# The entry into the decode loop and the order of its chunks, in a one-core layer of prompt and decode

## The chip, the cores and the metric

The kernel runs on one core of one Trainium2 chip. The time is the device time of a run in microseconds, as the median of several runs. Everything is float32.

## The reference, cut to what matters

One transformer layer is run for a prompt of 1024 tokens and for 8 decode sequences of 4 new tokens each with 2048 cached tokens. The heads are of two kinds: heads with a compressed, a selected and a window branch (NSA), and heads with a latent cache (MLA). The part that the change touches is the decode attention; the rest (projection, prompt attention, output projection) is around it.

```
full = concat([cache_nsa[page_table], kv_new])        # per sequence, 2048 + 4 rows of 4 x 2 x 64
kc, vc = compress(full[0], w_ck), compress(full[1], w_cv)    # 32 rows -> 1, every 16 rows
s   = q . kc * scale + bias;  p_c = softmax(s);  o_cmp = p_c . vc
imp = p_c . overlap;  idx = top_k(imp with forced blocks, 16)       # blocks of 64 rows
o_sel = softmax(q . k_selected + bias) . v_selected
o_win = softmax(q . [state_win, k_new] + bias) . [state_win_v, v_new]
o_lat = softmax(q_lat . ckv + q_rope . k_rope) . ckv   # latent cache, 2048 + 4 rows of 192
out = x + gate * (concat([(g0 o_cmp + g1 o_sel + g2 o_win) silu(z_a), (o_lat w_uv) silu(z_b)]) @ w_out)
y = rmsnorm(out) * g_final
```

## The kernel before, in words

The kernel is one program for five engines, each with its own instruction stream: TensorE (PE), VectorE (DVE), ScalarE (ACT), GpSimd (POOL) and SyncE (SP, which issues nearly all DMAs). The order on each engine is written out by hand, and engines wait for each other on semaphores only. An engine that waits holds up everything behind the wait in its own stream.

**The stages.** Projection of all tokens, preparation, prompt attention, the output projection of the eight prompt tiles (`pe_out`, `act_out`, `dve_out`, `pool_out`, `sp_out`, tiles m = 0 to 7), the decode loop over the sequences b = 0 to 7 (`pe_decode_loop` with its helpers, `act_decode`, `dve_decode`, `pool_decode`, `sp_decode`), and the output projection of the decode rows (`..._out_sample`).

**Output projection of a tile.** PE multiplies 32 blocks (L1609, two halves c of 512 columns, banks 2 to 5), DVE multiplies by the gate (L1692) and adds x (L1695), ACT squares and sums the row (L1672), POOL takes the inverse root (L1707, L1710), DVE scales (L1698), and SP stores the tile (L1577, the last tile L1581). In tiles 5, 6 and 7 PE also turns the first six of eight chunks of the first decode sequence (L1613). In this stage SP issues the loads that decode needs (L1559 to L1574).

**Chunks.** The keys and values to be compressed of one sequence are 16 pages of 128 rows. PE transposes four pages at a time into a PSUM bank (`chunk`, L1820: K0 to K3 for keys, V0 to V3 for values), and ACT or DVE copies the bank into `XT` (`read_chunk`, L2126; for ACT L2131 is the copy lambda, in the output stage L1662). The chunks K0, K2, V0, V2 are read by ACT, the others by DVE. In the loop, chunks of sequence b+1 and seven small results of sequence b (`cmp`, `pts`, `fmw`, `imp`, `smw`, `fs`, `ss`) go round three PSUM banks 0 to 2 in the order of `RING`; `next_bank` makes PE wait until the item three places back has been read. The first eight chunks use banks 6 and 7 in turn, with the wait two places back.

**One round of PE** (sequence b): `compress` of the keys (64 matmuls, L1965, banks 3 and 4), `window_scores` (L1978), `compressed_scores` (L1988), `latent_scores` 0 to 4 (L2000), `probabilities` (L2020 to L2022), `latent_scores` 4 to 6 (L2000, then L2004 to L2006), `compress` of the values 0 to 5, the sum over partitions `fmw` (L2031), `importance` (L2027), `compress` 5 to 16, `smw` (L2031), `selected_scores` (L2013), `latent_values` (L2037, L2041), `window_values` (L2048, L2049), `compressed_values` (L2054), K0 of b+1, `fs` (L2031), K1, K2, `ss` (L2031), K3, V0, V1, `selected_values` (L2059, L2061), V2, V3.

**One round of DVE.** It copies the output of the round before (L2204), turns the window keys into `KWT` (L2210) and the selected keys into `KT4` (L2215), subtracts masks from the window scores (L2222 to L2224), takes minima and spreads them (L2227, L2178; semaphore `s_nm` releases the sums `fmw` and `fs`), normalises the compressed probabilities (L2234 to L2236), copies `pts` (L2242), ranks blocks (L2252 to L2264), scales and turns probabilities (L2181, L2270, L2272), reads the compressed values (L2275), masks and reduces the selected scores (L2281 to L2287), reads `fs` (L2290), K1 (L2126), the latent result (L2294) and `ss` (L2297), scales and turns the selected probabilities into `PTS` (L2300), reads K3 and V1, turns the latent cache in three parts (`latent_turns`, L2173: `MLT0` to `MLT2`), and reads V3.

**The entry into decode.** Behind the output projection PE waits for both gated halves of the last tile (L1947), then turns V2 and V3 and compresses. `window_scores` of b = 0 waits for `KWT` turned, the query copies built by POOL (`QB`, L2364) and all late loads:

```
                if b == 0:
                    pe.wait_ge(s_late, LATE)
```

These late loads (`load_late`, L1872 to L1890) are 17 DMAs behind the last store: new keys into `KWT` (L1875), a mask (`NCBF`, L1879), `NEWM` (L1881), and the new values `VN` (L1886 to L1890). They wait for memsets that POOL does after the last tile (L2344 to L2346). DVE clears small tiles and adds two masks (L2183 to L2198), turns the latent cache, reads V3, and only then turns the window keys. SP reads the page numbers of b = 1 (`page_numbers`, a load of 16 registers, L1897) and issues its 16 pages (L1905) after the late loads.

## Time and profile before

| | us |
|---|---|
| median of three runs | 1207.02 (1205.22 to 1209.93) |
| the profiled execution, own time | 1206.63 |
| its span | 1204.9 |
| PE busy in the span | 1145.6 (95%) |
| DVE busy | 547.0 (45%) |
| ACT busy | 314.3 (26%) |
| GpSimd busy | 86.6 (7%) |

PE is the engine that is nearly always busy; the ends of its matmuls are modelled, so the start times of successive instructions are the surer reading. The output projection ends at 931 us on the clock of the span, the decode rounds run from 938 to 1190 us, about 30.6 us each.

### The profile page before, as it was taken

Reading aid. Unit: us, or ns where it says so; the run is one execution under the profiler, and the core shown is the slowest. Engines: PE = TensorE matmul, PEld = TensorE weight load, DVE = VectorE, ACT = ScalarE, POOL = GpSimd, SP = SyncE. Lnnn points to the kernel's source line nnn. Section 1 sums busy time; section 2 is a strip of 40 time slices with the busy share of each in tenths; the row PEclk is TensorE's granted clock in tenths of the full one; section 3 lists DMA queues with packets and bytes.
Section 4 is the critical chain, followed back from the end, with each engine's and each line's share of the span. In section 5 each row is a group of like instructions: output and inputs, shape, how many; then the busy total and the mean of one; then the engine's idle time right before and its main releaser. Section 6 shows DMA issues by size and latency. Waiting matters only on the chain.

```text
span 1204.9 us, 20843 instructions
## 1 busy us (share of the span) xinstructions
PE 1145.6 (95%) x7894; PEld 773.4 (64%) x7894; DVE 547.0 (45%) x1421; ACT 314.3 (26%) x636; POOL 86.6 (7%) x209
## 2 busy tenths in 40 slices
PE   5899999999999999998999999989999799999997
PEld 2576767444444667776888787864444576666665
DVE  0211110111111467767665655632333577777774
ACT  0212110101111356545443344420111122222220
POOL 0000000000000011101000000010000200000000
PEclk9799999999999989999999999999999899999998
DMA  9665212000003160000000000003961487666660
GB/s 346 258 204 145 106 35 85 10 7 4 3 7 42 32 164 2 2 1 2 1 1 1 1 1 1 2 12 110 211 222 52 159 266 260 225 221 226 222 180 19
DMA packets 83306, 115.94 MB, mean 96 GB/s; under 512 B 30113, under 2 KB 52052, under 8 KB 82184
## 3 DMA queue, kind: packets, MB, share of 16 engines
q1 hardware_dynamic: 83208, 114.61, 30.0%
q8 instruction: 64, 1.05, 0.4%
q14 instruction: 34, 0.28, 0.1%
HBM read 102.31 MB, written 12.27 MB: 95 GB/s over the span
## 4 chain that ended last, share of the span: by engine, by line
PE 81%; issue 8%; DVE 5%; DMA 3%; ACT 1%; SPq 1%; POOL 1%; POOLq 0%; DVEq 0%; ACTq 0%
PE PS L515 13%; PE PS L1331 11%; PE PS L1609 9%; PE PS L1362 7%; PE PS L1312 6%; PE PS L492 5%; PE PS L460 5%; PE PS L2000 3%; PE PS L1301 3%; PE PS L481 3%; DMA AR<-in_w_in 2%; PE PS L1965 2%; PE PS L2013 2%; PE PS L1308 2%; DVE AR L2173 1%
## 5 line engine op out<-in xcount | busy, mean ns | idle before, releaser
L1331 PE MATMUL PS<-AR 128*128 128x65 f32 (+1 forms) x1344 | 175.3, 271 | 0.7 <-DVE AR L1502 0.7
L1331 PEld LDWEIGHTS PS<-AR 128*128 128x128 f32 x1344 | 167.3, 194 | 0.9 <-issue 0.9
L515 PE MATMUL PS<-AR 128*128 128x512 f32 (+1 forms) x384 | 159.6, 575 | 2.7 <-DVE AR L767 2.7
L515 PEld LDWEIGHTS PS<-AR 128*128 128x128 f32 x384 | 72.3, 190 | 84.9 <-issue 81.2
L1382 ACT ACTIVATE AR<-PS,SM_ 128x64 f32<-128x64 f32 (+8 forms) x224 | 119.3, 594 | 26.9 <-DVE SM_ L1443 19.0
L1362 PE MATMUL PS<-CA,AR 128*128 128x128 f32 x704 | 117.0, 282 | 0.2 <-ACT AR L1382 0.2
L1609 PE MATMUL PS<-AR 128*128 128x512 f32 x256 | 111.7, 592 | 0.0
L1419 DVE TENSOR_REDUCE SM_<-PS 128x2 f32<-128x512 f32 (+6 forms) x62 | 58.9, 951 | 104.3 <-PE PS L1312 54.1
L1392 ACT ACTIVATE AR<-PS 128x512 f32<-128x512 f32 (+1 forms) x108 | 59.1, 547 | 176.1 <-PE PS L1362 175.7
L1362 PEld LDWEIGHTS PS<-CA,AR 128*128 128x128 f32 x704 | 80.8, 149 | 30.5 <-issue 20.9
L1609 PEld LDWEIGHTS PS<-AR 128*128 128x128 f32 x256 | 47.8, 190 | 55.9 <-issue 55.9
L1312 PE MATMUL PS<-AR 64*128 64x512 f32 (+3 forms) x384 | 74.9, 496 | 4.8 <-ACT AR L1382 4.8
L1965 PE MATMUL PS<-AR 64*128 64x128 f32 x1024 | 64.6, 279 | 0.0
L1401 DVE COPY AR<-PS 128x512 f32<-128x512 f32 (+1 forms) x100 | 57.8, 586 | 10.4 <-PE PS L1362 10.2
L1965 PEld LDWEIGHTS PS<-AR 64*128 64x128 f32 x1024 | 60.0, 190 | 2.2 <-issue 1.5
L492 PE MATMUL PS<-AR 128*64 128x128 f32 x1024 | 57.7, 273 | 0.0
L492 PEld LDWEIGHTS PS<-AR 128*64 128x64 f32 x1024 | 55.7, 137 | 2.8 <-issue 2.8
L460 PE MATMUL PS<-AR 128*128 128x512 f32 x128 | 56.3, 593 | 0.7 <-ACT AR L604 0.7
L1312 PEld LDWEIGHTS PS<-AR 64*128 64x128 f32 x384 | 32.2, 189 | 26.7 <-issue 17.4
L2131 ACT ACTIVATE AR<-PS 128x512 f32<-128x512 f32 x29 | 30.9, 1064 | 68.0 <-PE PS L1820 67.0
L1443 DVE CUSTOM_DVE_ANT_0 PS<-PS,AR,SM_ 128x256 f32<-128x256 f32 (+1 forms) x96 | 47.4, 535 | 1.7
L1820 PE MATMUL PS<-CA,AR 128*128 128x128 f32 x256 | 38.7, 283 | 9.8 <-ACT AR L2131 5.0
(337 smaller groups left out, 1347.1 us busy)
## 6 DMA issues: line engine op xcount, KB each, us to landing
AR<-in_cache_nsa SPq DMA_DIRECT2D x128, 256.0 KB, 5.0
AR<-in_cache_mla SPq DMA_DIRECT2D x128, 96.0 KB, 4.2
AR<-in_x_prompt SPq DMA_DIRECT2D x16, 512.0 KB, 4.4
AR<-in_w_ada SPq DMA_DIRECT2D x3, 2048.0 KB, 12.2
AR<-in_w_in SPq DMA_DIRECT2D x4, 1472.0 KB, 10.0
out<-AR SPq DMA_DIRECT2D x9, 512.0 KB, 3.0
AR<-in_w_ada SPq DMA_DIRECT2D x8, 512.0 KB, 5.9
AR<-in_w_out SPq DMA_DIRECT2D x4, 1024.0 KB, 9.7
```

Source lines behind the costliest of these rows:

```text
L460: mm = pe.matmul(PS[0:n, 3, :], ht(j, k)[:, 0:n], W1[:, k, 512:1024], start=(k == 0), stop=(k == KT - 1))
L492: mm = pe.matmul(PS[64 * g:64 * g + 64, 2, P * r:P * r + n], w1q(k, r, g), ht(j, k)[:, 0:n], start=(k == 0), stop=(k == KT - 1))
L515: mm = pe.matmul(PS[0:n, bank, 0:hi - lo], ht(j, k)[:, 0:n], w2cols(k, lo, hi), start=(k == 0), stop=(k == KT - 1))
L1312: mm = pe.matmul(scores(u, gi, o, o + P * n), QT[rg, r, q], keys[rg, ks], start=True, stop=True)
L1331: mm = pe.matmul(out, tile, v, start=(n == 0), stop=(n == nb - 1))
L1362: mm = pe.transpose(PS[:, 4 + c % 2, P * (t - t0):P * (t - t0) + P], tile(u, t), ident)
L1382: act.activation(probs(u, gi, 0, n), PSF[:, o:o + n], ACT.Exp, bias=NM[:, u % 2, gi:gi + 1], scale=-1.0).then_inc(s_exp, 1)
L1392: evac(act, c, lambda o, i: act.activation(o, i, ACT.Copy), s_evA)
L1401: copy(PTB[:, c % 4, 0:nt, :], PS[:, 4 + c % 2, 0:P * nt].rearrange("p (t q) -> p t q", t=nt)).then_inc(done, 1)
L1419: dve.tensor_reduce(nm, sc[:, :, 0:far], AX, ALU.min).then_inc(s_mx, 1)
L1609: mm = pe.matmul(PS[0:n, 2 + 2 * (m % 2) + c, :], YTO[m % 2][:, f, 0:n], weights[:, f, 512 * c:512 * c + 512], start=(f == 0), stop=(f == 7))
L1965: mm = pe.matmul(PS[:, 3 + g, 0:128], x if k else w, w if k else x, start=(l == 0), stop=(l == 15))
```

## The change

- The last tile's normalising step on DVE (`out_normed`) moves into round 0 of decode, and its store moves behind the page loads of b = 1 and the late loads.
- ACT reads its chunk of tiles 5 to 7 ahead of the square, not behind it.
- DVE's clears and mask additions (`decode_masks`) move to tile m = 4. `KWT` is cleared before the output projection, `NCBF` in tile m = 6.
- The loads into `KWT` and `NEWM` move into the load stage of tile m = 2. The mask `NCBF` is loaded first behind the output projection, then come the page numbers and pages of b = 1, and the `VN` loads follow them. Only `latent_values` of round 0 waits for `VN`.
- At the entry V3 goes to bank 0, PE waits for the first half of the last tile only, and the wait for the second half stands before `latent_scores`. DVE turns the window keys first, then the latent cache; V3 is read behind the window minima, and the selected keys of b = 0 are turned behind the compressed probabilities. In round 0 `latent_scores` 4 to 6 come before `probabilities`.
- In each round K0 of b+1 moves ahead of `selected_scores`; K2 and K3 of b+1 go to banks 3 and 4 and follow K1 at once; V2 moves ahead of `selected_values`. K3 is read by ACT. DVE turns the window keys of b+1 between V1 and V3, and the latent cache last.
- Some tiles move in SBUF so that this is possible.

```diff
-            m = at + len(tiles)
-            sp.wait_ge(s_yo, m)
-            sp.dma_start(y_t[tiles[-1]], YO[(m - 1) % 2][0:rows(tiles[-1]), :]).then_inc(s_out[(m - 1) % 2], 16)
...
+                if m >= 5:
+                    read_chunk(act, copy, 0, ("K0", "K2", "V0")[m - 5])
                 act.wait_ge(s_g2, 2 * m + 2)
                 if m >= 1:
                     act.wait_ge(s_so, m)
                 act.activation(JK[0:n, :], YO[m % 2][0:n, :], ACT.Square, accum_out=SSO[0:n, m:m + 1]).then_inc(s_so, 1)
-                if m >= 5:
-                    read_chunk(act, copy, 0, ("K0", "K2", "V0")[m - 5])
...
+        def out_normed(dve, m):
+            dve.wait_ge(s_ro, m + 1)
+            dve.scalar_tensor_tensor(YO[m % 2], YO[m % 2], RSO[:, m:m + 1], GF, ALU.mult, ALU.mult).then_inc(s_yo, 1)
...
+                if m < NT - 1:
+                    out_normed(dve, m)
+                if m == 4:
+                    decode_masks(dve)
...
+                if m == NT - 2:
+                    pool.wait_ge(s_po, 2 * NT - 2)
+                    pool.memset(NCBF, 0.0).then_inc(s_qd, 1)
...
-        MLT = [view(o, 1024).rearrange("p (j c) -> p j c", j=2) for o in (28032, 30080, 37248)]
+        MLT = [view(o, 1024).rearrange("p (j c) -> p j c", j=2) for o in (28032, 32128, 37248)]
         PTM = view(29056, 544).rearrange("p (n q) -> p n q", q=32)
-        KWT = view(32128, 768).rearrange("p (j c) -> p j c", j=4)
+        KWT = view(31104, 768).rearrange("p (j c) -> p j c", j=4)
...
-        NEWM = view(47200, 256).rearrange("p (b c) -> p b c", b=NB)
+        NEWM = view(31872, 256).rearrange("p (b c) -> p b c", b=NB)
...
-        OYS = view(31104, 1024).rearrange("p (b c) -> p b c", b=NB)
+        OYS = view(47520, 1024).rearrange("p (b c) -> p b c", b=NB)
...
-            RING += [(b, n) for n in SMALL_ITEMS[:5]]
-            ahead = [(b + 1, n) for n in CHUNK_ITEMS[0] + CHUNK_ITEMS[1]] if b + 1 < NB else []
-            RING += ahead[0:1] + [(b, "fs")] + ahead[1:3] + [(b, "ss")] + ahead[3:]
+            more = (lambda *names: [(b + 1, n) for n in names]) if b + 1 < NB else (lambda *names: [])
+            RING += [(b, n) for n in SMALL_ITEMS[:5]] + more("K0") + [(b, "fs")] + more("K1", "K2", "K3")
+            RING += [(b, "ss")] + more("V0", "V1", "V2", "V3")
+        SIDE = {(b, n): 3 + k for b in range(1, NB) for k, n in enumerate(("K2", "K3"))}
+        TURNS = [it for it in RING[FRONT:] if it not in SIDE]
+        TURN_AT = {it: m for m, it in enumerate(TURNS)}
         AT = {it: m for m, it in enumerate(RING)}
-        BY_ACT = {it: it[1] in ("K0", "K2", "V0", "V2") for it in RING}
+        BY_ACT = {it: it[1] in (("K0", "K2", "K3", "V0", "V2") if it[0] else ("K0", "K2", "V0", "V2")) for it in RING}
...
-        DT = ("MLT0", "MLT1", "MLT2", "KWT", "KT", "PTM", "PTW", "PTS")
+        DT = ("KWT", "MLT0", "MLT1", "MLT2", "KT", "PTM", "PTW", "PTS")
...
-            return PS[:, 6 + m % 2 if m < FRONT else m % 3, :]
+            if m < FRONT:
+                return PS[:, 0 if name == "V3" else 6 + m % 2, :]
+            return PS[:, SIDE[b, name] if (b, name) in SIDE else (TURN_AT[b, name] + 1) % 3, :]
...
-            back = 2 if m < FRONT else 3
-            if m >= back and not FRONT <= m < FRONT + 3:
-                wait_read(pe, *RING[m - back])
+            if m < FRONT:
+                if 2 <= m and name != "V3":
+                    wait_read(pe, *RING[m - 2])
+            elif (b, name) in SIDE:
+                pe.wait_ge(s_cv, 2 * b)
+            elif TURN_AT[b, name] == 2:
+                wait_read(pe, 0, "V3")
+            elif TURN_AT[b, name] > 2:
+                wait_read(pe, *TURNS[TURN_AT[b, name] - 3])
             return bank_of(b, name)
...
+            sp.wait_ge(s_qd, 8)
+            for k in range(2):
+                sp.dma_start(KWT[0:32, :, 128 + 32 * k:160 + 32 * k],
+                             ks_dram[k].rearrange("(j c) x -> c j x", c=32)).then_inc(s_nb, 16)
+            sp.dma_start(NEWM, cN.rearrange("p (b c) -> p b c", b=NB)).then_inc(s_nb, 16)
...
-        def load_late(sp):
-            sp.wait_ge(s_qd, 8)
-            for k in range(2):
-                sp.dma_start(KWT[0:32, :, 128 + 32 * k:160 + 32 * k],
-                             ks_dram[k].rearrange("(j c) x -> c j x", c=32)).then_inc(s_late, 16)
+        def load_mask(sp):
             sp.wait_ge(s_qd, 9)
             for t in range(TS):
                 sp.dma_start(NCBF[t:RS:TS, 119:127], U_dram[:, 142 - t:142 - t + 113:16],
-                             allow_slow_non_contiguous=True).then_inc(s_late, 16)
-            sp.dma_start(NEWM, cN.rearrange("p (b c) -> p b c", b=NB)).then_inc(s_late, 16)
+                             allow_slow_non_contiguous=True).then_inc(s_mask, 16)
+
+        def load_late(sp):
...
-        LATE = 16 * (2 + 4 + 1 + 10)
+        NB_EARLY = 16 * (24 + 14 + 3 + 8 + 1)
+        LATE = 16 * 10
...
-            load_late(sp)
+            load_mask(sp)
             for b in range(1, NB):
                 pages = page_numbers(sp, b)
+                if b == 1:
+                    sp.wait_ge(s_yT, NT)
                 load_pages(sp, b, pages, 0, NPG)
+                if b == 1:
+                    load_late(sp)
+                    sp.wait_ge(s_yo, NT)
+                    sp.dma_start(y_t[NT], YO[1]).then_inc(s_out[1], 16)
                 load_window(sp, b)
                 load_latent(sp, b, pages)
...
-            pe.wait_ge(s_g1, 16)
+            pe.wait_ge(s_g1, 15)
...
-                    for c in range(2, 4):
+                    for c in range(4):
...
-                if b == 0:
-                    pe.wait_ge(s_late, LATE)
-                else:
+                if b >= 1:
                     pe.wait_ge(s_o, 2 * b - 1)
...
+                    else:
+                        pe.wait_ge(s_g1, 16)
...
+                    if b == 0:
+                        pe.wait_ge(s_late, LATE)
...
+                if b == 0:
+                    latent_scores(b, 4, 6)
                 probabilities(b)
-                latent_scores(b, 4, 6)
+                if b >= 1:
+                    latent_scores(b, 4, 6)
...
+                ahead("K0")
                 selected_scores(b)
                 latent_values(b, 0, NPG)
                 window_values(b)
                 compressed_values(b)
-                ahead("K0")
                 if b == NB - 1:
...
-                ahead("K1")
-                ahead("K2")
+                for name in ("K1", "K2", "K3"):
+                    ahead(name)
...
-                for name in ("K3", "V0", "V1"):
+                for name in ("V0", "V1", "V2"):
                     ahead(name)
...
-                ahead("V2")
                 ahead("V3")
...
-                    for name in ("K2", "V0", "V2"):
+                    for name in ("K2", "K3", "V0", "V2"):
                         read_chunk(act, copy, b + 1, name)
...
+        def decode_masks(dve):
+            dve.memset(MK, 0.0)
+            dve.memset(SUM, 0.0)
...
+            dve.wait_ge(s_cst, 80)
+            dve.wait_ge(s_nb, NB_EARLY)
+            dve.wait_ge(s_gsb, 192)
+            dve.tensor_tensor(WBM[96:128, :].rearrange("p (j r) -> p j r", j=4),
+                              WBM[96:128, :].rearrange("p (j r) -> p j r", j=4),
...
+            dve.wait_ge(s_dv, 1)
...
-            dve.wait_ge(s_out[0], 64)
-            dve.wait_ge(s_out[1], 64)
-            dve.wait_ge(s_po, 16)
-            dve.memset(MK, 0.0)
...
-            dve.wait_ge(s_gsb, 176)
-            dve.tensor_tensor(WBM[96:128, :].rearrange("p (j r) -> p j r", j=4),
...
-            latent_turns(0)
-            read_chunk(dve, dve.tensor_copy, 0, "V3")
-            for b in range(NB):
-                if b >= 1:
-                    dve.wait_ge(s_avd, 8 * b)
-                    dve.tensor_copy(OYS[:, b - 1, :], O_B[:, 0:128]).then_inc(s_o, 1)
+            def window_turn(b):
...
+            def selected_turn(b):
                 dve.wait_ge(s_nsa[b % 2], 256 * (b // 2) + 256)
...
+            window_turn(0)
+            dve.wait_ge(s_so, NT)
+            latent_turns(0)
+            for b in range(NB):
+                if b >= 1:
+                    dve.wait_ge(s_avd, 8 * b)
+                    dve.tensor_copy(OYS[:, b - 1, :], O_B[:, 0:128]).then_inc(s_o, 1)
+                    selected_turn(b)
...
-                    dve.wait_ge(s_late, LATE)
+                    dve.wait_ge(s_mask, 64)
...
+                if b == 0:
+                    read_chunk(dve, dve.tensor_copy, 0, "V3")
...
+                if b == 0:
+                    out_normed(dve, NT - 1)
...
+                if b == 0:
+                    selected_turn(0)
+                    dve.wait_ge(s_out[0], 64)
...
-                    read_chunk(dve, dve.tensor_copy, b + 1, "K3")
                     read_chunk(dve, dve.tensor_copy, b + 1, "V1")
+                    window_turn(b + 1)
+                    read_chunk(dve, dve.tensor_copy, b + 1, "V3")
                     latent_turns(b + 1)
-                    read_chunk(dve, dve.tensor_copy, b + 1, "V3")
...
+            pool.memset(KWT, 0.0).then_inc(s_qd, 1)
...
-            pool.memset(KWT, 0.0).then_inc(s_qd, 1)
-            pool.memset(NCBF, 0.0).then_inc(s_qd, 1)
             pool.memset(VN, 0.0).then_inc(s_qd, 1)
```

## Rows read from the trace of the kernel before

**Rows 1.** Waits of PE, 700 to 1205 us: engine line waited for, total us, times, longest.

```profile
PE PS L1820 <- ACT AR L2131: 5.0, 14, 0.4
PE PS L1978 <- DVE AR L2210: 4.8, 7, 0.7
PE PS L1978 <- DMA AR<-out: 4.5, 1, 4.5
PE PS L1820 <- ACT AR L1662: 3.3, 1, 3.3
```

**Rows 2.** Timeline of PE at the entry: start us, length us, engine, line, operation [idle before].

```profile
931.23 0.60 PE L1820 MATMUL PS<-CA,AR 128*128 128x128 f32 x4
...
938.29 4.80 PE L1965 MATMUL PS<-AR 64*128 64x128 f32 x64
947.63 2.90 PE L1978 MATMUL PS<-AR 128*128 128x192 f32 x8 [4.54 <-DMA AR<-out]
950.46 1.09 PE L1988 MATMUL PS<-AR 128*32 128x127 f32 x8
...
959.49 0.39 PE L2031 MATMUL PS<-AR,CE 128*128 128x8 f32 x2
```

**Rows 3.** Windows: stretch, length, busy us of each engine (x instructions), PEclk, DMA share, GB/s.

```profile
947.60:950.50 2.90, 2.87 (x9) 2.46 (x10) 0.00 (x0) 0.00 (x0) 0.00 (x0) 0.50 0.00 0
```

**Rows 4.** Timeline of DVE at the entry.

```profile
932.15 0.69 DVE L1695 TENSOR_TENSOR AR<-AR 128x512 f32<-128x512 f32 x1
...
936.17 1.01 DVE L2126 COPY AR<-PS 128x512 f32<-128x512 f32 x1
...
940.11 3.50 DVE L2173 STREAM_TRANSPOSE AR<-AR 128x1024 f32<-128x1024 f32 x3
...
944.37 0.67 DVE L2210 STREAM_TRANSPOSE AR<-AR 128x512 f32<-128x512 f32 x1
944.96 2.27 DVE L2215 STREAM_TRANSPOSE AR<-AR 128x2048 f32<-128x2048 f32 x1
```

**Rows 5.** Timeline of GpSimd at the entry.

```profile
936.51 0.75 POOL L2364 TENSOR_TENSOR AR<-AR,CE 128x128 f32<-128x128 f32 x2
```

**Rows 6.** Timeline of the SP queue: issues of DMAs.

```profile
945.69 0.32 SPq L1890 DMA_DIRECT2D AR<-out  x1
951.49 8.65 SPq L1905 DMA_DIRECT2D AR<-in_cache_nsa  x16
```

**Rows 7.** The page loads of decode (L1905), 940 to 1100 us: from issue to landing.

```profile
DMA to landing us min/median/max: 2.6/4.8/6.6
```

**Rows 8.** Timeline of PE in one decode round and into the next.

```profile
999.31 0.39 PE L2031 MATMUL PS<-AR,CE 128*128 128x4 f32 x2
...
1001.19 0.38 PE L2031 MATMUL PS<-AR,CE 128*128 128x2 f32 x2
...
1002.38 1.09 PE L1820 MATMUL PS<-CA,AR 128*128 128x128 f32 x8 [0.32 <-ACT AR L2131]
1003.41 0.30 PE L2059 MATMUL PS<-AR 128*32 128x128 f32 x1
...
1005.64 3.84 PE L1965 MATMUL PS<-AR 64*128 64x128 f32 x64
1010.16 1.57 PE L1978 MATMUL PS<-AR 128*128 128x192 f32 x8 [0.68 <-DVE AR L2210]
...
1023.87 0.38 PE L2031 MATMUL PS<-AR,CE 128*128 128x2 f32 x2
1024.11 3.68 PE L2013 MATMUL PS<-AR 128*128 128x512 f32 x8
```

**Rows 9.** Timeline of DVE in the same round.

```profile
997.39 0.64 DVE L2281 TENSOR_TENSOR AR<-PS,AR 128x480 f32<-128x480 f32 x1
...
1002.55 0.74 DVE L2300 STREAM_TRANSPOSE AR<-AR 128x544 f32<-128x544 f32 x1
...
1012.23 0.25 DVE L2222 TENSOR_TENSOR AR<-PS,CE 128x128 f32<-128x128 f32 x1
```

More of the change, by code:

```diff
@@ L401, in sp_projection @@
                 .then_inc(s_wu, 16)
-            sp.wait_ge(s_gs, 16)
+            sp.wait_ge(s_gsb, 16)
             for h in range(H):
@@ L1866, in load_gates @@
         def load_gates(sp):
-            sp.wait_ge(s_gsb, 128)
+            sp.wait_ge(s_gsb, 144)
             for i in range(1, 4):
@@ L2151, in act_decode @@
                 if b + 1 < NB:
-                    for name in ("K2", "V0", "V2"):
+                    for name in ("K2", "K3", "V0", "V2"):
                         read_chunk(act, copy, b + 1, name)
+        def decode_masks(dve):
+            dve.memset(MK, 0.0)
+            dve.memset(SUM, 0.0)
+            dve.memset(PC[0:RS, :], 0.0)
+            dve.memset(PG[0:RS, :], 0.0)
+            dve.wait_ge(s_cst, 80)
[3 more added lines that the diff above has]
+                              WBM[96:128, :].rearrange("p (j r) -> p j r", j=4),
+                              TMPW[96:128, :].rearrange("p (r j) -> p j r", j=4), ALU.add)
+            new = WBN[0:RS, :].rearrange("p (b c) -> p b c", c=36)[:, :, 0:4]
+            dve.tensor_tensor(new, new, NB15[0:RS, 32:36].rearrange("p (o c) -> p o c", o=1)
+                              .to_broadcast([RS, NB, 4]), ALU.add).then_inc(s_dv, 1)
+            dve.wait_ge(s_dv, 1)
         def dve_decode(dve):
-            count = [0]
+            count = [1]
             def step(ins):
@@ L2181, in scale @@
                 step(dve.tensor_scalar(buf[:, 0:cols], buf[:, 0:cols], RCD[:, c:c + 1], None, ALU.mult))
-            dve.wait_ge(s_out[0], 64)
-            dve.wait_ge(s_out[1], 64)
-            dve.wait_ge(s_po, 16)
-            dve.memset(MK, 0.0)
-            dve.memset(SUM, 0.0)
-            dve.memset(PC[0:RS, :], 0.0)
-            step(dve.memset(PG[0:RS, :], 0.0))
-            dve.wait_ge(s_cst, 80)
-            dve.wait_ge(s_nb, NB_EARLY)
-            dve.wait_ge(s_gsb, 176)
-            dve.tensor_tensor(WBM[96:128, :].rearrange("p (j r) -> p j r", j=4),
-                              WBM[96:128, :].rearrange("p (j r) -> p j r", j=4),
-                              TMPW[96:128, :].rearrange("p (r j) -> p j r", j=4), ALU.add)
-            new = WBN[0:RS, :].rearrange("p (b c) -> p b c", c=36)[:, :, 0:4]
-            step(dve.tensor_tensor(new, new, NB15[0:RS, 32:36].rearrange("p (o c) -> p o c", o=1)
-                                   .to_broadcast([RS, NB, 4]), ALU.add))
-            latent_turns(0)
-            read_chunk(dve, dve.tensor_copy, 0, "V3")
-            for b in range(NB):
-                if b >= 1:
-                    dve.wait_ge(s_avd, 8 * b)
-                    dve.tensor_copy(OYS[:, b - 1, :], O_B[:, 0:128]).then_inc(s_o, 1)
+            def window_turn(b):
                 dve.wait_ge(s_wn[b % 2], 16 * (b // 2) + 16)
```

12 lines of the change are left out of this document (4 added, 8 removed).

## The prediction

> **What bounds the kernel now.** I read the page first: PE is busy for 95% of the span, so a gain has to come out of PE's own time or out of its last gaps. Next the waits of PE over the second half [rows 1]: 4.5 us once at `window_scores` for a DMA, 3.3 us once at the chunk V2 for ACT, and, in every decode round, a wait for the window keys (4.8 us in 7) and two for ACT's chunk reads (5.0 us in 14). Then the timelines, for what stands around these gaps. At the entry [rows 2] the last chunk of the output stage (V1) starts at 931.23 and `compressed_scores` of round 0 only at 950.46: 19.2 us for three chunks, one `compress` and one `window_scores`. The clock is part of it: `window_scores` runs with a granted clock of 0.50, the 1.2 GHz level [rows 3], and takes 2.90 us against 1.57 us in a warm round; `compress` takes 4.80 against 3.84 us [rows 2, 8]. What holds the entry is seen on the other engines. DVE adds the last tile at 932.15, but it turns the window keys at 944.37, behind the last scaling, a V1 read, the masks, the latent turns of 3.50 us and V3 [rows 4]; and the last of the late loads is issued at 945.69 [rows 6], after which PE goes on at 947.63.
>
> **The entry.** All starts below are compared with the row of the same instruction before.
> - PE: two chunks take 1.03 us from start to start (1002.38 to 1003.41) [rows 8], so one is 0.51. V2 now needs the V0 read, which ACT does ahead of its square and so some 7 us earlier than it needs to be; V3 has a free bank. V1, V2, V3 end at 931.23 + 3 x 0.51 = 932.76, `compress` at 936.60 (3.84), `window_scores` at 938.17 (1.57), both at the full clock since PE no longer stands still. Gain: 950.46 - 938.17 = 12.3 us.
> - Is `window_scores` free at 936.60? DVE: add ends 932.84, V1 read 1.01, window turn 0.67 [rows 4]: 934.5, early by 2 us. Before, QB was built at 936.51 + 0.75 = 937.26 behind three clears, two of which (0.9 us together in POOL's stream, my estimate) are gone; it lies between 0 and 0.66 us late [rows 5], and I take 0.1. The new keys of `KWT` are loaded a hundred us earlier.
> - `latent_scores` 0 to 4 start a `compressed_scores` later, near 939.2. The latent turns end at 934.5 + 3.50 = 938.0, so they are in time.
> - DVE in round 0, from 938.2: masks and the first minima 1.5 us, V3 read 1.0, the compressed minimum 0.3, the moved scaling of the last tile 1.3, the normalising 0.8, the selected turn 2.27 [rows 4], the small ones estimates from their like in the same trace: 945.4. PE in the meantime does both parts of `latent_scores`, which now stand before `probabilities`, and reaches `fmw` at 938.17 + (959.49 - 950.46) = 947.2 [rows 2]. `fmw` needs DVE's copy of `pts` and a minimum behind it, about 1.3 us after `probabilities`, beside 1.3 us of `compress`: I take 0.2 us of new wait, with 0 and 1 as ends.
> - SP: the mask loads need `NCBF` cleared (tile 6, about 920.5) and are issued from 922 to 925. Page numbers take 951.49 - 946.01 = 5.5 us and the 16 pages 8.65 us [rows 6], so pages of b = 1 go out from 930.5 to 939.2, the ten `VN` loads until 943.5. With the longest landing, 6.6 us [rows 7], all is in SBUF by 950.1. K0 of b = 1 comes at 947.2 + 2.6 + 0.2 = 950.0 and needs pages only (945.8); `latent_values` needs `VN` and comes not before 950.0 + 0.5 + 3.6 = 954.1.
> - The rest costs nothing. The mask additions in tile 4 (about 1 us of DVE) and the three loads in tile 2 (1.7 us of SP) lie beside 14.6 us of matmuls per tile, of which DVE uses 4 to 6 us; the next x tile has over 4 us of slack. If that cover were gone, it would be 1 to 2 us once. Last store: behind it SP has some 250 us.
>
> Entry: 12.3 - 0.1 - 0.2 = 12.0 us, with ends 12.3 and 10.6 (12.3 - 0.66 - 1).
>
> Against the page "SBUF — State Buffer" of the Trainium skill, section "Who interferes with whom": a DVE instruction with two SBUF inputs and a GpSimd instruction that reads SBUF exclude each other for a whole instruction. The scaling that moves into round 0 has two SBUF inputs, and POOL builds the queries of b = 1 at that time. By the page DVE would start up to one build later (two take 0.75 us [rows 5]), which reaches PE with at most 0.4 us, and the sum would be 1188.4 in place of 1188.0. The trace of before shows no such pair long enough to tell.
>
> **A round.** There are seven transitions b to b+1. From `fs` (999.31) to the next `compress` (1005.64) PE takes 6.33 us, and until `window_scores` 4.52 us more [rows 8].
> - K0 ahead of `selected_scores` moves their end by 0.51. It was at 1024.11 + 3.6 = 1027.7, and DVE's subtraction started at 997.39 + 30.58 (the period) = 1027.97 [rows 8, 9], so it had 0.25 us to spare and is now late by 0.3. `fs` hangs on that chain (1.92 us from 997.39 to 999.31): it starts at 999.61. New wait: 0.3 us.
> - Behind it: `fs` takes 0.24 (1023.87 to 1024.11), K1, K2, K3 without a wait 1.54, so `ss` is at 1001.39. `PTS` was turned at 1002.55 + 0.74 = 1003.29, 2.10 after `ss` at 1001.19 [rows 8, 9]; it is now turned at 1003.49, and `selected_values` starts at 1003.6. PE with V0, V1, V2 is there at 1001.39 + 0.24 + 1.54 = 1003.17 and waits 0.4. `selected_values` 1.20 (1005.64 - 1003.41 - 1.03), V3 0.51: `compress` starts at 1005.31. Gain 0.33 us.
> - `compress` takes 3.84 and `window_scores` stood 0.68 us behind it [rows 8]. The window keys are now turned between V1 and V3, about 5 us ahead. Gain 0.68 us.
> - What is late next: DVE ends the latent turns and the selected turn at about 1012.2, where it began with the masks before [rows 9], and PE comes to `probabilities` 1.0 us earlier than it did, at about 1015.3. DVE needs 2.6 us from 1012.2: 1014.8. It fits by 0.5 us.
> - ACT reads K3 as well (1 us); it idles for most of the round, and V3's bank is read 0.8 us before it is wanted.
> - K0 asks for its pages 4.6 us earlier in the round. SP may issue them when `selected_values` of the round before last ends (about 1004.6); issue 8.65 and longest landing 6.6 [rows 6, 7] give 1019.9, and K0 comes at 1024.1 - 1.0 = 1023.1. 3.2 us to spare.
>
> Round: 1.0 us, seven times 7.0. Ends: if neither new wait appears, 0.7 more, 1.7 us; if DVE's chain is slower than I place it, 0.3 us. The last round and the tail have no chunks and gain nothing.
>
> **Sum.** 12.0 + 7.0 = 19.0 us. The profiled execution took 1206.63 us (span 1204.9), which is 0.4 below the median of 1207.02; from the median it is 1188.0. With the ends: 24.2 us (12.3 + 7 x 1.7) gives 1182.8, 12.7 us (10.6 + 7 x 0.3) gives 1194.3.
>
> **The rivals.**
> - *DVE takes over in the rounds.* `fs` and `PTS` already end within 0.1 us of PE, and the order K1, K2, K3, `ss` leaves DVE only one chunk read before them. If each is 0.3 to 0.4 us later than computed, only 0.3 us a round is left: 12.0 + 2.1 = 14.1 us, 1192.9. Against it: DVE loses one chunk read of 1.0 us per round. 12%.
> - *The entry is held by a late load.* `VN` now stands behind 4 MB of pages. Were it to land 5 us later than placed, at 955, and then another 4, `latent_values` would stop PE for about 4 us, and the time is 1192. For it: the DMA engines are full while pages come. Against it: the longest landing seen is 6.6 us. [...] 4%.
> - *The entry doesn't do what it says*: some wait of `window_scores` stays as late as before, and only the rounds gain: 1200. For it: five waits stand there; against it: each of them was placed above. 2%.
> - *Slower: K0 stops PE for its pages.* PE is in order, so K0 ahead of `selected_scores` holds everything behind it if the pages are late. It has 3.2 us to spare by the longest landing. To lose 19.0 us in seven rounds takes 2.7 us each, so the last page would have to land 5.9 us later than that, 12.5 us from its issue; a us more, and it is 1214. Around the break-even point lies the case of no difference. 2% slower, 2% within 0.5%.
>
> **How the numbers follow.** My forecast has 78%, the others as given. All but the last are over 0.5% (6 us, about what a measurement of this kernel can tell from none) faster: faster 96%, same 2%, slower 2%. Time 1188; the range from 1183 to 1196 takes in both ends of the sum and the first two rivals.
>
> **What would show it.** `window_scores` of round 0 near 936.7 with a full clock; no wait of PE over 0.5 us between 931 and 950; `fmw` near 947.4; a period of 29.6 us; a wait of about 0.3 us at `fs` and about 0.4 us at `selected_values` in its place; none at `window_scores` and at K2 and K3. The forecast is wrong if the period stays above 30.2 or K0 waits for a DMA.

## The result and the profile after

The changed kernel takes 1184.61 us (median of 4 runs, 1183.92 to 1188.34), the kernel before 1207.18 us (4 runs). The ratio is 0.9823, with a 95% interval of 0.9801 to 0.9846: 21.4 us faster, between 18.6 and 24.0. Forecast were 1188.0 us (range 1183 to 1196) and a gain of 19.0.

The profiled execution took 1183.95 us, 22.7 less than that of before. Line numbers are those of the changed file. From its page:

```profile
span 1182.2 us, 20859 instructions
...
PE 1138.3 (96%) x7894; PEld 770.8 (65%) x7894; DVE 541.8 (46%) x1414; ACT 319.7 (27%) x643; POOL 86.5 (7%) x209
...
PEclk9899999999999999999999999999999999999997
```

PE has 7.3 us less of busy time with the same instructions. Of this 3.3 us lie in the entry, where the granted clock was 0.83 on average before and is 1.00 now, and 4.9 us in the seven transitions of rounds, where it was 1.00 before and after (ahead of the entry it has 0.8 us more). The transitions, before and then after (stretch, length, busy us by engine, clock, DMA share, GB/s):

```profile
950.50:1164.60 214.10, 204.31 (x2088) 148.99 (x2088) 162.54 (x358) 49.31 (x91) 11.62 (x30) 1.00 0.69 230
```

```profile
936.10:1141.80 205.70, 199.38 (x2087) 149.07 (x2086) 161.18 (x354) 54.25 (x98) 13.90 (x36) 1.00 0.70 232
```

So in the rounds it is not the clock. A wait there costs more than its row lists, because the modelled tail of the matmul ahead of it counts as busy: before, K1 starts at 999.56 and K2 at 1000.58, 1.02 us later, where chunks in a row stand 0.45 apart, and the row lists 0.39 of these 0.57 us:

```profile
1000.58 0.66 PE L1820 MATMUL PS<-CA,AR 128*128 128x128 f32 x4 [0.39 <-ACT AR L2131]
```

PE's waits behind 900 us (engine, line, what it waited for: us in total, times, longest):

```profile
PE PS L2085 <- DVE AR L2341: 4.8, 8, 1.5
PE PS L2055 <- DVE AR L2222: 3.0, 7, 0.5
PE PS L1629 <- ACT AR L1633: 1.7, 1, 1.7
```

All four waits of [rows 1], at the chunks and at the window scores, are gone, and the two that were forecast stand in their place: at `fs` (L2055, 3.0 us in 7) and at the selected values (L2085, 4.8 us in 8; 1.5 of it in the last round, as before).

**The entry** on PE, which answers to [rows 2]; then DVE's turn of the window keys and SP's pages and last `VN` load, for [rows 4] and [rows 6]:

```profile
929.32 1.47 PE L1836 MATMUL PS<-CA,AR 128*128 128x128 f32 x12
930.73 3.84 PE L1989 MATMUL PS<-AR 64*128 64x128 f32 x64
934.66 1.54 PE L2000 MATMUL PS<-AR 128*128 128x192 f32 x8
936.13 1.05 PE L2010 MATMUL PS<-AR 128*32 128x127 f32 x8
...
945.10 0.39 PE L2055 MATMUL PS<-AR,CE 128*128 128x8 f32 x2
```

```profile
931.76 0.69 DVE L2233 STREAM_TRANSPOSE AR<-AR 128x512 f32<-128x512 f32 x1
932.36 3.46 DVE L2217 STREAM_TRANSPOSE AR<-AR 128x1024 f32<-128x1024 f32 x3
```

```profile
929.15 8.84 SPq L1923 DMA_DIRECT2D AR<-in_cache_nsa  x16
...
941.36 0.32 SPq L1908 DMA_DIRECT2D AR<-out  x1
```

V1, V2 and V3 run as one group of 12 (the first row), and the rows list no wait until `fmw`. From V1's start to the compressed scores it is 6.81 us in place of 19.23, and to `fmw` 15.78 in place of 28.26. The granted clock of the window scores is 1.00, against 0.50 in [rows 3]:

```profile
934.60:937.10 2.50, 2.44 (x16) 2.06 (x16) 2.01 (x7) 0.47 (x1) 2.32 (x6) 1.00 1.00 333
```

**A round** on PE, for [rows 8], from two neighbouring rounds; below it DVE's rows for [rows 9]:

```profile
984.15 0.39 PE L2055 MATMUL PS<-AR,CE 128*128 128x4 f32 x2 [0.45 <-DVE AR L2222]
...
985.74 0.31 PE L2055 MATMUL PS<-AR,CE 128*128 128x2 f32 x2
985.91 1.51 PE L1836 MATMUL PS<-CA,AR 128*128 128x128 f32 x12
987.87 0.30 PE L2085 MATMUL PS<-AR 128*32 128x128 f32 x1 [0.46 <-DVE AR L2341]
...
989.67 3.84 PE L1989 MATMUL PS<-AR 64*128 64x128 f32 x64
993.44 1.57 PE L2000 MATMUL PS<-AR 128*128 128x192 f32 x8
...
1007.15 0.38 PE L2055 MATMUL PS<-AR,CE 128*128 128x2 f32 x2
1007.39 0.64 PE L1836 MATMUL PS<-CA,AR 128*128 128x128 f32 x4
...
1013.56 0.39 PE L2055 MATMUL PS<-AR,CE 128*128 128x4 f32 x2 [0.45 <-DVE AR L2222]
```

```profile
983.69 0.40 DVE L2222 TENSOR_SCALAR AR<-CE,AR 128x4 f32<-128x4 f32 x1
...
987.07 0.74 DVE L2341 STREAM_TRANSPOSE AR<-AR 128x544 f32<-128x544 f32 x1
...
996.45 0.26 DVE L2256 TENSOR_TENSOR AR<-PS,CE 128x128 f32<-128x128 f32 x1
```

The period is 29.41 us in place of 30.58. The gap from `compress` to the window scores fell from 4.52 to 3.77; from `smw` to `fs` it grew from 6.02 to 6.41, since K0 now stands in it; from `fs` to the next `compress` it fell from 6.33 to 5.52. The wait at `fs` is shorter in the last transition: GpSimd (POOL) has no further queries to build there, DVE's spread ahead of `fs` takes 0.23 us in place of 0.40, and the transition takes 29.24 us in place of 29.39 to 29.42:

```profile
1130.75 0.23 DVE L2222 TENSOR_SCALAR AR<-CE,AR 128x4 f32<-128x4 f32 x1
1131.03 0.39 PE L2055 MATMUL PS<-AR,CE 128*128 128x4 f32 x2 [0.28 <-DVE AR L2222]
```

**Where the time went**, cut at V1's start and at the compressed scores of rounds 0 and 7:

| stretch | before | after | gain | forecast |
|---|---|---|---|---|
| start to V1 | 931.23 | 929.32 | 1.91 | 0 |
| V1 to compressed scores of round 0 | 19.23 | 6.81 | 12.42 | 12.2 |
| seven transitions of rounds | 214.11 | 205.69 | 8.42 | 6.8 |
| from there to the end | 40.33 | 40.38 | -0.05 | 0 |
| span | 1204.9 | 1182.2 | 22.7 | 19.0 |

The forecast put 0.2 us of its entry at `fmw`, which lies in the line of the seven transitions here. The first line isn't the change's. Both executions are at the same instruction 424 us into the span to within 0.8 us, and in the next 16 us the one of before got a clock of 0.74 and the other 1.00, in code that is the same:

```profile
424.00:440.00 16.00, 14.62 (x73) 10.46 (x72) 7.19 (x40) 8.22 (x26) 1.44 (x6) 0.74 0.89 229
```

```profile
424.00:440.00 16.00, 13.88 (x95) 9.56 (x94) 9.92 (x48) 9.96 (x32) 1.43 (x6) 1.00 0.85 204
```

So 20.8 us are the change's own in these two executions, and the experiments below are read by stretches inside decode, which this doesn't touch: in every kernel the transitions between rounds 1 and 6 agree within 0.03 us, while the medians of the few runs of each carry up to some 4 us from ahead of decode.

### The profile page after: what moved, and what is told of

It is laid out like the page before. It is cut to its first block, busy times and chain, and to the rows that moved or that the text cites. A ratio compares the mean times of both kernels' runs of the same rounds, so it can differ in the third digit from the quotient of the medians.

```text
span 1182.2 us, 20859 instructions
## 1 busy us (share of the span) xinstructions
PE 1138.3 (96%) x7894; PEld 770.8 (65%) x7894; DVE 541.8 (46%) x1414; ACT 319.7 (27%) x643; POOL 86.5 (7%) x209
## 4 chain that ended last, share of the span: by engine, by line
PE 84%; issue 8%; DVE 3%; DMA 2%; ACT 1%; SPq 1%; POOL 0%; POOLq 0%; ACTq 0%; DVEq 0%
PE PS L515 13%; PE PS L1331 11%; PE PS L1606 9%; PE PS L1362 7%; PE PS L1312 6%; PE PS L492 5%; PE PS L460 5%; PE PS L1989 4%; PE PS L2024 3%; PE PS L1301 3%; PE PS L481 3%; DMA AR<-in_w_in 2%; PE PS L2037 2%; PE PS L1308 2%; PE PS L895 1%
## 5 line engine op out<-in xcount | busy, mean ns | idle before, releaser
L1362 PE MATMUL PS<-CA,AR 128*128 128x128 f32 x704 | 116.1, 280 | 0.2 <-ACT AR L1382 0.2
L1606 PE MATMUL PS<-AR 128*128 128x512 f32 x256 | 111.7, 592 | 0.0
L460 PE MATMUL PS<-AR 128*128 128x512 f32 x128 | 56.3, 593 | 0.7 <-ACT AR L604 0.7
L1514 POOL TENSOR_TENSOR AR<-AR 128x256 f32<-128x256 f32 x32 | 23.2, 726 | 338.5 <-DVE AR L1502 338.5
L2024 PE MATMUL PS<-AR 128*128 128x512 f32 x96 | 45.2, 609 | 0.0
```

The costliest lines, as they stand in the source:

```text
L460: mm = pe.matmul(PS[0:n, 3, :], ht(j, k)[:, 0:n], W1[:, k, 512:1024], start=(k == 0), stop=(k == KT - 1))
L1362: mm = pe.transpose(PS[:, 4 + c % 2, P * (t - t0):P * (t - t0) + P], tile(u, t), ident)
L1606: mm = pe.matmul(PS[0:n, 2 + 2 * (m % 2) + c, :], YTO[m % 2][:, f, 0:n], weights[:, f, 512 * c:512 * c + 512], start=(f == 0), stop=(f == 7))
L2024: pe.matmul(S_B, QM[b % 2][:, j, :, :].rearrange("p i q -> p (i q)"), MLT[j // 2][:, j % 2, :], start=(j == 0), stop=(j == 5))
```

## The experiments

All edit the changed kernel. "Entry" is the time from V1's start to the compressed scores of round 0 (6.81 us), "period" the distance of two rounds (29.41 us); the run of before has 19.23 and 30.58.

**e1, the entry alone** (rounds as before, or so it was meant), and **e5**, which puts back the one step that e1 had left changed.

```diff
-            RING += ... more("K0") + [(b, "fs")] + more("K1", "K2", "K3")   ... SIDE = {K2, K3: banks 3, 4}
+            RING += ... more("K0") + [(b, "fs")] + more("K1", "K2")         ... SIDE = {}
# PE: K0 behind compressed_values, K3 behind ss, V2 behind selected_values; K3 read by DVE
# DVE: window_turn(b) at the start of round b
# e5 only:
-                    read_chunk(dve, dve.tensor_copy, b + 1, "V3")
                     latent_turns(b + 1)
+                    read_chunk(dve, dve.tensor_copy, b + 1, "V3")
```

> The changed kernel with the order inside the rounds as before (K0 behind the compressed values, K2 and K3 in the ring of three banks, K3 read by DVE, V2 behind the selected values, window keys turned at the start of the next round); the entry stays changed. Theory (entry and rounds are two separate gains, 12.4 us and seven times 1.17 us by the two traces): from V1's start to the compressed scores of round 0 still 6.8 us, the period again 30.6 us, time about 1184.6 + 8.2 = 1193 us. Rival (the rounds are shorter because the loads run earlier after the changed entry, not because of their order): the period stays near 29.4 us and the time near 1185 us.

Measured: 1197.83 us (ratio to before 0.9935, 0.9913 to 0.9957), entry 6.81, period 31.37. Neither the theory's period nor the rival's: it is longer than before's. The rival, that the earlier loads shorten the rounds, is out, but the edit didn't restore the rounds.

> The kernel of the run before (entry changed, rounds as before) with one more step put back, which that run had left changed: DVE turns the latent cache of b+1 ahead of its read of V3, not behind it. Theory (its period of 31.37 us came from V3's read, which waits for PE, standing ahead of 3.45 us of turns while the window keys still come last): the period is again 30.6 us, and with an entry of 6.8 us the time is 1184.6 + 8.2 = 1193 us. Rival (the changed loads also shorten or lengthen the rounds): a period off 30.58 by more than 0.1 us.

Measured: 1193.33 us (0.9888, 0.9866 to 0.9911), entry 6.81 (929.09 to 935.90), period 30.58. The waits of PE in e1 and then in e5:

```profile
PE PS L2001 <- DVE AR L2235: 10.3, 7, 1.5
PE PS L1837 <- ACT AR L2161: 5.0, 14, 0.4
```

```profile
PE PS L1837 <- ACT AR L2161: 5.0, 14, 0.4
PE PS L2001 <- DVE AR L2235: 4.8, 7, 0.7
PE PS L1629 <- ACT AR L1633: 1.7, 1, 1.7
```

e5 has the very waits of [rows 1] in its rounds. Entry and rounds are separate gains, and e5's rival, a period off by more than 0.1 us, is out. And e1 shows what one place on DVE is worth: V3's read must wait for PE, and 3.45 us of turns behind it make the window keys 0.8 us later in each round.

**e11, e2, e4: the edits of the rounds one by one.** e11 is e5 with the new order on DVE; e2 has K0 ahead of the selected scores as well; e4 is the changed kernel with K0 alone put back.

```diff
# e11, against e5: DVE turns the window keys between V1 and V3, the latent cache last
# e2, against the changed kernel: SIDE = {}, K3 by DVE and behind ss, V2 behind selected_values
# e4, against the changed kernel:
-                ahead("K0")
                 selected_scores(b)
                 latent_values(b, 0, NPG)
                 window_values(b)
                 compressed_values(b)
+                ahead("K0")
```

> The kernel of run e5 (entry changed, rounds as before) with the window keys of b+1 turned between V1 and V3 and the latent cache last: the one edit of the rounds that is left is the order on DVE. Theory (the gains of the rounds add up: this one 0.75 us, the side banks 0.4 us, K0 nothing): period 29.85 to 29.9 us, time 1187.5 to 1188.5 us. Rival (the edits need each other, since K3's read on DVE delays V3 and the latent turns, which then end late for the latent scores or the probabilities): period over 30.1 us.

> The changed kernel with K2 and K3 of b+1 back in the ring of three banks, K3 read by DVE and V2 behind the selected values; K0 stays ahead of the selected scores and the window keys stay turned early. Theory (the part from fs to the next compress, 6.33 us before and 5.52 us after, is shorter because K2, K3 and V0 no longer wait for reads in the ring): it goes back to about 6.3 us, minus what K0 gives, as K0 is read early here: 6.0 to 6.3 us; period 29.9 to 30.2 us, time 1188 to 1190 us. Rival (the ring's waits were only shadows of the wait for the turned selected probabilities, which bounds this part anyway): the part stays at 5.5 to 5.7 us and the period at 29.4 to 29.6 us, time 1185 to 1186 us.

> The changed kernel with K0 of b+1 back behind the compressed values. Theory (K0 ahead of the selected scores delays them and so fs by 0.4 us, but behind the compressed values its read stands on ACT ahead of the exponential and delays ss by as much: both orders bound the selected values at the same point): fs comes 0.4 us earlier in the round, ss and the selected values within 0.1 us of where they are, period 29.3 to 29.5 us, time 1184 to 1186 us. Rival (the new wait at fs is a pure loss that the other edits pay for): the period falls by 0.4 us to 29.0 us, and the time by 2.8 us to 1182 us.

Measured: e11 1187.39 us, period 29.82; e2 1187.65 us, period 29.82; e4 1185.28 us, period 29.34. So the order on DVE gives 30.58 - 29.82 = 0.76 us a round. The side banks, with ACT's K3 and with V2's move (these three were not taken apart), give 0.48 without K0's move (e11 to e4) and 0.41 with it (e2 to the changed kernel). e11 and e2 fell just short of their theories' 29.85 and 29.9, and the rivals of all three are out. The reason given for e2 was wrong: the chunks' waits for reads in the ring (5.0 us in 14) are there in e11 and not in e2, where PE waits 0.45 us at `fs`, 0.20 at `ss` and up to 0.2 at the selected values, and the part from `fs` to `compress` takes 5.94 us. Moving K0 gives nothing without them (e11 and e2) and costs 0.07 with them (e4 and the changed kernel). The gains add up. Why K0 is nearly neutral is seen in e4, on PE and on ACT:

```profile
1012.73 0.39 PE L2055 MATMUL PS<-AR,CE 128*128 128x4 f32 x2
...
1014.61 0.38 PE L2055 MATMUL PS<-AR,CE 128*128 128x2 f32 x2
```

```profile
1012.90 1.07 ACT L2159 ACTIVATE AR<-PS 128x512 f32<-128x512 f32 x1 [7.57 <-PE PS L1836]
1013.76 0.71 ACT L2162 ACTIVATE AR<-AR 128x544 f32<-128x544 f32 x1
```

`fs` is ahead by 0.39 us (6.02 behind `smw`), but ACT is reading K0 when DVE has read `fs` (1013.31), the exponential starts 0.4 us later than it could (in the changed kernel it starts 0.04 us behind that read), and `ss` comes 1.88 us behind `fs` in place of 1.59.

**e3, the window keys late** in the changed kernel.

```diff
                     read_chunk(dve, dve.tensor_copy, b + 1, "V1")
-                    window_turn(b + 1)
                     read_chunk(dve, dve.tensor_copy, b + 1, "V3")
                     latent_turns(b + 1)
 ...
                     dve.tensor_copy(OYS[:, b - 1, :], O_B[:, 0:128]).then_inc(s_o, 1)
+                    window_turn(b)
                     selected_turn(b)
```

> The changed kernel with DVE turning the window keys of b+1 at the start of the next round, behind the copy of the round's output, as before. Theory (the 0.75 us between the end of compress and the window scores came from this order alone): the gap from compress to window scores is again about 4.5 us in place of 3.77 us. The latent turns now follow V3 and the window turn comes last but one on DVE, so it ends about 0.6 us later than the latent turns do now; window scores wait 0.9 to 1.0 us, period 30.2 to 30.5 us, time 1190 to 1192 us. Rival (PE would lose the time later in the round anyway, at the probabilities): the period stays within 0.2 us of 29.4 us, time 1184.6 to 1186 us.

Measured: 1198.11 us, period 30.94, a wait of 1.5 us at the window scores in each round (10.3 us in 7). The direction is the theory's, the size was underrated: in the changed kernel the latent turns end 0.7 us after the window scores start (994.14 against 993.44), and the copy of the output and the turn itself, 0.9 us together, now stand behind them. The rival, that the time is lost later anyway, is out.

**e6, the late loads first.**

```diff
             load_mask(sp)
+            load_late(sp)
             for b in range(1, NB):
 ...
                 if b == 1:
-                    load_late(sp)
                     sp.wait_ge(s_yo, NT)
 ...
# window_scores:
+                if b == 0:
+                    pe.wait_ge(s_late, LATE)
```

> The changed kernel with the ten loads of new values issued ahead of the page numbers and pages of b = 1, and waited for at the window scores of round 0, as before. Theory (this wait is what held the entry before; the pages come on time only because they go first): the loads can go from 933.4 us, when their tile is cleared, and land about 1.9 us behind their last issue, near 939.5; window scores of round 0 start there in place of 934.7, so 4.8 us later, and the part after the wait starts at a lower clock, 1 to 1.5 us more. The pages of b = 1 are issued from about 943.4 to 952.2 us and land near 955 to 958, where K0 of b = 1 is now due at 954.8: 1 to 3 us of wait for the pages. Time 1184.6 + 6 to 9 = 1190.5 to 1193.5 us, period unchanged. Rival (the values land early anyway and only DVE's order held the entry): window scores within 1 us of 934.7, time within 1 us of 1184.6.

Measured: 1195.38 us, 10.8 over the changed kernel; from V1 to the compressed scores of round 0 it takes 11.55 us in place of 6.81, and to those of round 1 47.60 in place of 36.20; the later periods are 29.41. On PE, and the clock of two of the stretches:

```profile
938.25 2.49 PE L2002 MATMUL PS<-AR 128*128 128x192 f32 x8 [3.88 <-DMA AR<-out]
940.67 1.73 PE L2012 MATMUL PS<-AR 128*32 128x127 f32 x8
...
957.04 1.09 PE L1836 MATMUL PS<-CA,AR 128*128 128x128 f32 x4 [3.14 <-DMA AR<-in_cache_nsa]
957.92 5.91 PE L2039 MATMUL PS<-AR 128*128 128x512 f32 x8
```

```profile
938.20:940.60 2.40, 2.35 (x8) 2.01 (x8) 0.00 (x0) 0.00 (x0) 0.15 (x1) 0.60 0.00 0
...
958.00:963.70 5.70, 5.70 (x9) 2.15 (x8) 0.00 (x0) 1.03 (x1) 0.00 (x0) 0.60 1.09 349
```

Both waits came where the theory put them, 3.8 us at the window scores and 3.1 at K0 for the pages of b = 1. The size was missed by 2 to 5 us, because I had charged the lower clock once and not behind the second wait: the selected scores take 5.9 us at 0.60 in place of 3.6. Here the forecast's rival of the slower side is real: K0 ahead of the selected scores does stop PE when the pages come late.

**e9, ACT's read behind the square; e10, the masks back.**

```diff
# e9, act_out
-                if m >= 5:
-                    read_chunk(act, copy, 0, ("K0", "K2", "V0")[m - 5])
                 act.wait_ge(s_g2, 2 * m + 2)
 ...                                       # square
+                if m >= 5:
+                    read_chunk(act, copy, 0, ("K0", "K2", "V0")[m - 5])
# e10, dve_out and dve_decode
-                if m == 4:
-                    decode_masks(dve)
 ...
+            decode_masks(dve)
             window_turn(0)
```

> The changed kernel with ACT reading its chunk of tiles 5 to 7 behind the square again. Theory (V2 can't be turned before V0 has been read; this order alone holds PE for 3.3 us and lets its clock fall): V0's read ends near 933.1, V2 starts there in place of 929.8, 3.4 us later, and what follows starts at the lower clock, 1.6 to 2.7 us more (from the two waits of the run with the late loads first). From V1's start to the compressed scores 11.8 to 12.9 us in place of 6.8, time about 1190 us. Rival (PE keeps its clock over a gap of 3 us): 10.2 us, time 1188 us.

Measured: 1189.62 us; entry 11.74 us, 4.93 more than in the changed kernel: a wait of 3.28 us and 1.7 us of slower matmuls:

```profile
935.54 1.79 PE L1836 MATMUL PS<-CA,AR 128*128 128x128 f32 x8 [3.28 <-ACT AR L1659]
937.26 4.71 PE L1989 MATMUL PS<-AR 64*128 64x128 f32 x64
```

> The changed kernel with DVE's clears and mask additions back behind the last tile, ahead of its turn of the window keys. Theory (the 1.0 us that they take lay in slack, the window keys being turned 2.2 us before PE needs them): window scores of round 0 at most 0.1 us later, the masks' subtraction 0.6 us later on DVE and absorbed before the probabilities; time and entry as in the changed kernel, 1184.6 us within 1 us. Rival (DVE is the bound of the entry by now): from V1's start to fmw 0.6 to 1.0 us more.

Measured: 1187.41 us. The trace gives 0.25 to the edit (V1 to `fmw` 16.03 in place of 15.78); of the 4.5 us by which its profiled execution (1188.45) is slower, 4.0 lie ahead of V1, which starts at 933.36 here. Not DVE's time costs it but POOL's: PE's row lists a wait of 0.35 us for the query copies. The rows are PE's, POOL's and DVE's:

```profile
938.96 1.54 PE L1998 MATMUL PS<-AR 128*128 128x192 f32 x8 [0.35 <-POOL AR L2403]
```

```profile
936.25 0.45 POOL L1707 TENSOR_SCALAR SM_<-SM_ 128x1 f32<-128x1 f32 x1 [13.64 <-ACT AR L1671]
...
942.03 0.82 POOL L2407 TENSOR_TENSOR AR<-AR,CE 128x384 f32<-128x384 f32 x1
```

```profile
936.24 0.40 DVE L2190 TENSOR_TENSOR CE<-CE,AR 32x128 f32<-32x128 f32 x1
...
941.96 0.91 DVE L2220 TENSOR_SCALAR AR<-CE,AR 128x4 f32<-128x4 f32 x1
```

**e7, e8 and e12: a better order.** The chain from the selected scores over DVE, `fs`, ACT and `ss` to the turned probabilities bounds the selected values. e7 fills PE's wait with V3, e12 takes K0 off the chain, e8 does both.

```diff
# e7: V3 in bank 5 (free once DVE has subtracted: s_rd), ahead of selected_values
-        SIDE = {... enumerate(("K2", "K3"))}
+        SIDE = {... enumerate(("K2", "K3", "V3"))}
+                pe.wait_ge(s_rd if name == "V3" else s_cv, 2 * b)        # next_bank
+                        wait_read(pe, b, "V3")                         # latent_scores, b >= 1
-                for name in ("V0", "V1", "V2"):
+                for name in ("V0", "V1", "V2", "V3"):
                     ahead(name)
# e12: K0 behind selected_scores, ahead of latent_values; e8: both
-                ahead("K0")
                 selected_scores(b)
+                ahead("K0")
```

> The changed kernel with V3 of b+1 put in bank 5, the bank of the selected scores, which is free once DVE has subtracted from it; PE turns V3 ahead of the selected values and so in the time in which it waits for the turned probabilities. Theory (the 0.47 us wait there is bound by DVE's chain, not by PE's own work, so work moved into it is free): the period falls by 0.45 us to 28.95 us, the time by 3.2 us to about 1181.5 us. Rival (DVE is by now just in time at the probabilities of the next round, so that the gain comes back as a wait there): a wait of PE at the probabilities, period 29.2 to 29.4 us, time 1183.5 to 1184.6 us.

> The changed kernel with K0 of b+1 between the selected scores and the latent values and nothing else. Theory (K0's two old places each put 0.3 to 0.4 us on the chain that bounds the selected values, one at its start, one on ACT; this place is free of both, so it gains what it gained beside the moved V3, 0.39 us of 28.83): period 29.0 us, time 1184.6 - 2.7 = 1182 us. Rival (it gained there only because V3 ahead of the selected values had made the chain the sole bound): period 29.3 to 29.4 us, time 1184 us.

> The same with K0 of b+1 between the selected scores and the latent values. Theory (the chain from the selected scores over DVE, fs, ACT and ss to the turned probabilities bounds the selected values; K0 ahead of it delays its start by 0.45 us of which DVE takes back 0.2, and K0 at its end stands in ACT's way; between the two it costs nothing): the chain starts 0.26 us earlier than in the run beside it, period 28.7 us, time about 1179.7 us. Rival (K0's place is worth nothing, as the run with K0 behind the compressed values showed 0.07 us): period as in the run beside it, time as there.

Measured: e7 1182.21 us (0.9782, 0.9758 to 0.9806), period 28.82; e12 1182.75 us (0.9793, 0.9773 to 0.9813), period 29.03; e8 1177.41 us (0.9759, 0.9738 to 0.9780), period 28.44. Gains per round 0.59, 0.38 and 0.97: they add up, and all three rivals are out. Moving V3 gave more than the wait of 0.47 us that it fills, because in its old place behind the selected values it took 0.59 us (989.08 to 989.67); so e7 came out below the expected 28.95. In e8 K0's place gave 0.38 us beside it where 0.26 was expected; 0.11 of it is that DVE's spread now takes 0.29 us beside POOL's build in place of 0.40. This makes the 28.44 in place of 28.7. e8 beats both kernels; PE has no wait left in its rounds, only that of the last round and the one in the tail:

```profile
PE PS L1629 <- ACT AR L1633: 1.7, 1, 1.7
PE PS L2086 <- DVE AR L2341: 1.5, 1, 1.5
```

## Why the prediction was right

- **Bound and gaps.** Right: all of the gain is PE's, in its gaps and, in the entry alone, in its clock.
- **The entry, 12.0 forecast, 12.5 measured (28.26 - 15.78, up to `fmw`).** Undone alone in the changed kernel, ACT's read costs 4.9 us of it (e9), the late loads 4.7 (e6, 11.55 against 6.81) and the masks 0.3 (e10). The further 6.7 us of e6 come from the pages of b = 1 behind the late loads, which stop K0 in its new place. DVE's order of turns at the entry, V3's own bank and the wait for the first half only were not undone alone, so that they were holds is argued from the rows and not shown.
- **The two small waits of the entry.** Both came, below what the rows list. The window scores start 3.93 us behind the start of `compress` in place of 3.77 in a round, 0.16 later (0.1 forecast), and 0.14 us behind the end of the query copies (933.76 + 0.76). In e10 the copies end 0.26 us later behind V1 and the window scores again start 0.14 behind them: the query copies hold the entry by now. `fmw` starts 1.49 us behind its `compress` in place of 1.32, 0.17 later (0.2 forecast), which the latent scores made up, as they run in one go (7.48 us from the compressed scores to `compress` in place of 7.71).
- **Chunks.** I took 0.51 us each. They take 0.45 to 0.47 (12 matmuls from 984.39 to 985.74). The pair that I measured, 1002.38 to 1003.41, ends with the start of the selected values, whose weight load waited 0.17 us for the turned probabilities. This is 0.12 us of the entry; another 0.17 is that I took `compress` and the window scores by the lengths of their rows (3.84 and 1.57), though their starts stand 3.77 and 1.47 to 1.50 from what follows.
- **A round, 1.0 forecast, 1.17 to 1.20 measured.** Window keys 0.68 forecast, 0.75 measured. `fs` later by 0.3 forecast, 0.39 measured. From `fs` to `compress` 0.63 forecast (0.33 net of `fs`), 0.81 measured, 0.19 of it from the three chunks K1 to K3; the wait at the selected values 0.4 forecast, 0.47 shown. Of the 0.39 us at `fs` 0.12 is not K0's but POOL's, a term that the sum didn't have: DVE's spread takes 0.40 us in the changed kernel (983.69) and 0.28 in e4, and 0.23 in the last transition, where POOL stands still.
- **What is late next.** Right: DVE starts its masks at 996.45, 6.8 behind the start of `compress`, and PE waits nowhere for the probabilities.
- **A slip.** K0 asks for its pages 5.3 us earlier in the round than before (1029.37 against 1024.11), not 4.6. The time to spare was worked out from its start and not from this.
- **Costs at nothing.** Right: the last four tiles of the output projection up to V1 take 59.75 us, 59.76 before, with the masks and the loads moved into this stage. e10 shows that the masks would cost 0.25 us at their old place.
- **The rivals.** DVE taking the rounds over, and an entry held by a late load, did not come: the latent values of round 0 start at 952.56 with no wait listed, and no row shows when `VN` landed. The slower one was real as a mechanism (e6), and its slack was enough in the changed order. What the first line of the table adds, 1.9 us, is chance and no merit of the forecast.

The page "SBUF — State Buffer" of the Trainium skill, section "Who interferes with whom", which the prediction weighed, says that a DVE instruction with two SBUF inputs, or in a mode with two ports, and a GpSimd instruction that reads SBUF exclude each other. e10 agrees: POOL's first step beside DVE's mask addition takes 0.45 us (0.19 in the changed kernel), and DVE's spread beside POOL's build of 0.82 us takes 0.91 (0.23 alone); which of the two kinds the spread is, no run shows. The spread of each round (0.40 beside a build, 0.23 without) looks like the same effect: at 983.69 the spread ends with POOL's build (984.09 and 984.07). It costs the changed kernel 0.17 us in each of six transitions. The scaling that moved into round 0 was not hit, as POOL was done by then (938.79 against 937.73 + 0.83); the 0.4 us that the prediction made of the page for it did not come. One build is up to 0.83 us, more than the two of 0.75 together that it went by.

## What to carry to other kernels

Where several engines hold one entry, take every hold away in one go, and price the clock with each wait: here a gap of 3.1 to 3.9 us cost 1.6 to 2.7 us more in the matmuls behind it (e9, e6). In a loop bound by a chain over several engines, put independent work of the busy engine neither ahead of the chain nor where its reader blocks a link of it, but right behind the chain's first step, and fill the final wait from a free bank. When an edit is undone to test it, check the restored part against the old trace: e1 had one step wrong and its period told it.

## What was not expected

- The scatter of the runs is made ahead of decode. V1 starts between 929.0 and 933.7 us in the thirteen profiled executions of the changed kernel and its variants, in which all code ahead of the output projection is the same. In the 16 us behind 424 us the granted clock is 0.70 to 0.75 in the five in which V1 starts at 931.1 or later and 1.00 in the eight in which it starts by 929.3. This is as much as the side banks are worth. Why the clock is low there in some executions stays open.
- The slower matmuls come behind a wait, and not always at once. In e9 V2 and V3, right behind the wait of 3.28 us, are slow at once (1.72 us in place of 0.94, granted clock 0.56), and the window scores run at full speed again 6.4 us later. In the kernel before, V2 behind a wait of 3.26 us at the same place ran at 1.00 (0.63 us), and V3 behind a further wait of 1.53 us at 0.50 (1.12 us).
